# A hybrid decoder layer on one core: eight instead of six row pairs by Strassen's seven products in the first half of each down product

## The chip, the cores and the metric

The kernel runs on one core of a Trainium2 chip. The metric is the device time of one execution in microseconds, from the first to the last instruction with what lies around them; the median of several runs is compared. TensorE does the matrix products, VectorE and ScalarE the elementwise work, GpSimd (POOL in the profile) and SyncE (SP) issue transfers. Each engine takes its own instructions in the order in which they are written.

## The reference

One layer of a decoder for 256 tokens of width 2048, in fp32. What matters here are its two feed-forward blocks:

```
h = h + 0.5 * rmsnorm(swiglu(rmsnorm(h, n_pre), w_gu, w_down), n_post)

def swiglu(x, w_gu, w_down):
    g, u = split(x @ w_gu, 2)
    return (silu(g) * u) @ w_down
```

w_gu is 2048 x 11264 and w_down 5632 x 2048. Between the two blocks stands a mixer (gated linear attention, gated delta rule and cross-attention to 256 memory tokens), which the change does not touch.

## The kernel before, in words

**Units.** A weight matrix is read in units: 256 rows by 512 columns, 512 KB, which land in one of eight places of `raw`. ScalarE rounds a unit into `whi` (L1289, four places), VectorE subtracts that from `raw` and leaves the rest in `wlo` (L1823 for one unit, L1971 for two at once; `wlo` lies over `raw`). Activations are held in the same two parts. An fp32 product is then three matmuls: high by high, high by low, low by high (L858).

**Pairs.** The down product makes 256 tokens x 2048 columns from 5632 = 44 x 128 rows. Its first half makes columns 0 to 1023, the second half the rest. In the first half the rows are taken as 22 pairs (pair q: row blocks 2q and 2q+1), and a pair has two units, one for each 512 columns. In a plain pair, `eight` in the code, the 2 x 2 blocks of activations and the 2 x 2 blocks of weights give eight block products of 128 x 128 x 512, 24 matmuls. In a pair named in `DOWN_AT`, `seven` in the code, they are combined after Strassen: seven block products, 21 matmuls. For that VectorE must form three sums of weight blocks (`weight_sums`, L1959 to L1964, into `wsum`; the third changes a block of `raw` in place), which are rounded and split like a unit (`wsum_hi` L1419, `wsum_lo` L1986), and four sums of activation blocks (`down_sides`, L2110 to L2117, by way of `down_a` into `down_side`), which ScalarE rounds (`down_hi`, L1497) and VectorE splits (`down_sides_lower`, L2122). `down_hi` and `down_lo` keep a place for every seven of the product.

The gate-up products are built alike, with sevens at pairs 2, 4 and 6 of eight (`SEVEN_AT`); their activation sums are made once for all, and not in every step.

**Order.** The order is written out by hand. While TensorE works on unit j (slot j; slots 2q and 2q+1 belong to pair q), the other engines prepare unit j+4, that is pair q+2. ScalarE in slot j waits until unit j is used, rounds unit j+4, and after the rounding of an even slot may do `down_hi`. VectorE splits both units of a plain pair together in the odd slot. The sums for a seven at pair q fall as follows:

```
down_sides(q)         VectorE, slot 2(q-3), ahead of the split of pair q-1
down_hi               ScalarE, slot 2(q-3), behind the first rounding of pair q-1
down_sides_lower      VectorE, slot 2(q-3)+1, behind the split of pair q-1
weight_sums(q)        VectorE, slot 2(q-2), once the preceding seven has used wsum
splits, wsum_lo(q)    VectorE, slots 2(q-2) and 2(q-2)+1
```

In slot 9 VectorE also makes the low part of the last activations (L2066). After the last seven, ScalarE copies the first product out of its bank (`copy_first`, L1426) into the token buffer `nat`, and VectorE combines the banks there.

**The last half.** The second half of the first down product uses plain units only. The second half of the second one takes its pairs in `LAST_ORDER`, the first 14 as pairs, with sevens at places 2, 4, ... 12 of that order (`LAST_AT`), and uses the `down_hi` and `down_lo` that the first half left.

Of the kernel before, what the change touches and what calls it, by code (L numbers as in the profile page):

```python
# [8 lines left out]
SEQ = 256  # L9
P = 128  # L10
NT = SEQ // P
D_FF = ((8 * D // 3 + 255) // 256) * 256
CW = 512
UK = 2
# [33 lines left out]
N_GU = D_FF // CW  # L48
# [39 lines left out]
TURN_AT, UPPER_AT, LOWER_AT = 4, 11, 12  # L88
SEVEN_AT = (2, 4, 6)
N7 = len(SEVEN_AT)  # L90
DOWN_AT = (4, 7, 10, 13, 16, 19)
D7 = len(DOWN_AT)
SIDES_AHEAD = 3
LAST_ORDER = (0, 1, 4, 2, 7, 3, 10, 5, 13, 6, 16, 8, 19, 9, 11, 12, 14, 15, 17, 18, 20, 21)
LAST_PAIRS = 14
LAST_AT = tuple(LAST_ORDER.index(k) for k in DOWN_AT)
LAST_REST = U_F - LAST_PAIRS
LAST_GATE = 2 * LAST_PAIRS + LAST_REST
SPLIT_SMALL = 20
# [9 lines left out]
def hybrid_layer(nc, a, out, h_dram, mk_dram, mv_dram):  # L109
    fp32 = mybir.dt.float32  # L110
    f32r = mybir.dt.float32r
# [6 lines left out]
    with ExitStack() as ctx:  # L118
# [22 lines left out]
        def sem(name):  # L141
            if name not in sems:
                sems[name] = ctx.enter_context(nc.semaphore(name))
            return sems[name]
# [7 lines left out]
        def in_group(name, g=0):  # L152

            if name in ACT_GROUP:
# [4 lines left out]
        ov = overlay([("raw", [P, RAW, UK, CW], fp32)], [("wlo", [P, RAW, UK, CW], f32r)])  # L159
        raw, wlo = ov["raw"], ov["wlo"]  # L160
        ov = overlay(
            [("act_hi", [P, KT_F, SEQ], f32r), ("act_lo", [P, KT_F, SEQ], f32r)],
            [("u_hi", [P, KT_D, SEQ], f32r), ("u_lo", [P, KT_D, SEQ], f32r),
             ("o_hi", [P, 3, KT_O, SEQ], f32r), ("o_lo", [P, 3, KT_O, SEQ], f32r),
             ("msum", [P, NT, CW], fp32), ("mtmp", [P, NT, CW], fp32)],
            [("below", [P, 2 * KT_D, SEQ], fp32), ("mkn", [P, NT, CW], fp32), ("mvn", [P, NT, CW], fp32),
             ("mkT", [P, 4, SEQ], fp32), ("wsm", [P, KT_D, 32], fp32), ("wsm2", [P, KT_D, 64], f32r),
             ("small_T", [64, SEQ], fp32)],
            [("below_post", [P, 80, SEQ], fp32), ("post_a", [P, 2, CW], fp32)],
# [21 lines left out]
             ("mkh", [P, 2, SEQ], fp32), ("mvh", [P, 2, 256], fp32)],  # L191
            [("zbh", U4, f32r), ("zbl", U4, f32r), ("gap", [P, 8, P], fp32), ("sqh", [P, 8, P], f32r)],
            [("sql", [P, 8, P], f32r)],
            [("down_hi", [P, D7, 4, P], f32r), ("down_lo", [P, D7, 4, P], f32r), ("down_a", [P, 2, UK, SEQ], fp32),
             ("down_side", [P, 2, 4, P], fp32)],
            [("res_ffn2", [P, NT, D], fp32), ("post_ffn2", [P, D], fp32)])
        zbh, zbl, sqh, sql = (ov[k] for k in ("zbh", "zbl", "sqh", "sql"))
        x_hi, x_lo = ov["x_hi"], ov["x_lo"]
        down_hi, down_lo, down_a, down_side = (ov[k] for k in ("down_hi", "down_lo", "down_a", "down_side"))
        m_turned, m_swapped = ov["m_turned"][:, :], ov["m_swapped"][:, :]  # L200

        block_res, block_post = (None, res_mix, ov["res_ffn2"]), (None, post_mix, ov["post_ffn2"])
# [6 lines left out]
        ov = overlay(  # L209
            [("nat", [P, NT, D], fp32), ("res", [P, 2, NT, CW], fp32)],  # L210
            [("pr", [P, 4, NT, CW], fp32), ("yr", [P, 10, SEQ], fp32)],
            [("gates", [P, 6, NT, CW], fp32)],
            [("below_wsum", [P, NT, D], fp32), ("wsum", [P, 3, CW], fp32), ("wsum_hi", [P, 3, CW], f32r)],
            [("below_norms", [P, 26, SEQ], fp32), ("gnorm", [P, GLA_DV], fp32), ("dnorm", [P, GDN_D], fp32)],
            [("below_side", [P, NT, D], fp32), ("below_side2", [P, 3, CW], fp32), ("side", [P, N7, 4, P], fp32)],
            [("below_wsl", [P, NT, D], fp32), ("wsum_lo", [P, 3, CW], f32r)])
        nat, res, pr, yr, gates = (ov[k] for k in ("nat", "res", "pr", "yr", "gates"))
        wsum, wsum_hi, wsum_lo = ov["wsum"], ov["wsum_hi"], ov["wsum_lo"]
        gnorm, dnorm, side = ov["gnorm"], ov["dnorm"], ov["side"]

        turned, swapped = nat[:, 0, D // 2:D], nat[:, 1, D // 2:D]

# [8 lines left out]
        def gate_t(t, h=0):  # L231
            return nat[:, t, 2 * h * CW:(2 * h + 1) * CW]
# [4 lines left out]
        def last_unit(j):  # L237

            if j < 2 * LAST_PAIRS:
                return LAST_ORDER[j // 2], j % 2  # L240
            c, r = divmod(j - 2 * LAST_PAIRS, LAST_REST)
            return LAST_ORDER[LAST_PAIRS + r], c

# [21 lines left out]
        def halves(v, l, h):  # L265
# [42 lines left out]
        ov = overlay([("junk", [P, CW], mybir.dt.bfloat16)], [("lrT", [RANK, SEQ], fp32)],  # L308
                     [("last_side_hi", [P, P], f32r), ("last_side_lo", [P, P], f32r)])
# [47 lines left out]
        def at(base, i, per, j):  # L357

            return base + i * per + j
# [9 lines left out]
        def sevens(f, i, s, per, j):  # L369

            if isinstance(i, int) and i > N_GU:
                return (f * ((N_GU - 1) * N7 + D7) + (N_GU - 1) * N7 + D7 * (i - N_GU) + s) * per + j
            return at((f * ((N_GU - 1) * N7 + D7) - N7) * per, i, N7 * per, s * per + j)
# [171 lines left out]
        def _(pl):  # L545
# [31 lines left out]
            for l in range(7):  # L577
                m = 1 << l
# [9 lines left out]
            for l in range(1, 7):  # L588
                m = 1 << l
# [157 lines left out]

            for n in range(N_GU, 2 * N_GU):
                swap_act(n)
            pl.wait_ge(sem("sum_used"), sevens(1, N_GU + 1, D7 - 1, 1, 1))  # L750
            fetch_block(2, a["n_ffn2_post"])
            rsqrt(R_D2, True, 0)
            rsqrt(R_D2, True, 1)
# [3 lines left out]
        def _(pe):  # L757
# [166 lines left out]
            def down_pairs(f, second=False):  # L924
# [21 lines left out]
                if f and second:  # L946
                    pair_stage(f, N_GU + 1, LAST_PAIRS, lambda j: base + 2 * U_F + j, act_hi, act_lo, LAST_AT, side_of,
                               LAST_ORDER, 2 * U_F, False)
                    for j in range(2 * LAST_PAIRS, 2 * U_F - SKEW):
# [7 lines left out]
                pe.wait_ge(sem("act_lo"), (f + 1) * N_GU)  # L957
                pair_stage(f, N_GU, U_F, lambda j: base + j, act_hi, act_lo, DOWN_AT, side_of)

# [317 lines left out]
        def _(ac):  # L1277
# [143 lines left out]
            def copy_first(f, i, n, h=0):  # L1421

                ac.wait_ge(unit_used, n + 1)
                if h == 0:
                    ac.wait_ge(sem("product"), at(f * N_GU, i, 1, 0))
                act(gate_t(0, h), mix[:, 0, :], ACT.Copy).then_inc(sem("first_copied"), 1)  # L1426

            def quads(f, i):
# [21 lines left out]
            def down(f):  # L1450
                n0, q = UB[f"down{f + 1}"], QB[f"down{f + 1}"] // 2

                def tasks(j):
# [15 lines left out]
                    if f == 1 and i == 1 and j in (5, 8):  # L1469

                        ac.wait_ge(acc_out[j // 8], q + 1)
                        squares(R_D2, j // 8, nat[:, :, j // 8 * CW:(j // 8 + 1) * CW])
                    if f == 1 and i == 1 and j == 2 * LAST_AT[-1]:
                        copy_first(f, N_GU + 1, n0 + 2 * U_F + j, 1)
# [16 lines left out]
                for j in range(2 * U_F):  # L1491
                    split_pairs(f, N_GU, DOWN_AT, n0 + j, (0, n0, 2 * U_F), j)
                    tasks(j)
                    if j % 2 == 0 and j // 2 + SIDES_AHEAD in DOWN_AT:
                        e = DOWN_AT.index(j // 2 + SIDES_AHEAD)
                        ac.wait_ge(sem("side"), 5 * (D7 + 1) * f + 5 * (e + 2))
# [7 lines left out]
                for j in range(2 * U_F):  # L1504
                    if j + LOOK < 2 * U_F:
                        split_pairs(f, N_GU + 1, LAST_AT, n0 + 2 * U_F + j, (0, n0, 2 * U_F), j)
                    tasks(j)
# [308 lines left out]
        def _(ve):  # L1816
# [171 lines left out]
            def first_sums(f, i, s, h):  # L1988

                ve.wait_ge(sem("sum_used"), sevens(f, i, s, 1, 1))  # L1990
                ve.wait_ge(sem("first_copied"), per_chunk(f, i, 1, 1))
                tt(up_t(0, h), mix[:, 2, :], gate_t(0, h), ALU.subtract).then_inc(sem("combined"), 1)
                ve.wait_ge(sem("combined"), per_chunk(f, i, 4, 1))
                tt(gate_t(1, h), mix[:, 3, :], up_t(0, h), ALU.add).then_inc(sem("combined"), 1)
# [138 lines left out]
            def last_tasks(j):  # L2133

                n0, q, i = UB["down2"] + 2 * U_F, QB["down2"] // 2, N_GU + 1
                if j == 2 * LAST_AT[-1] + 2:
                    first_sums(1, i, D7 - 1, 1)
                if j == 2 * LAST_AT[-1] + 3:
                    ve.wait_ge(sem("combined"), per_chunk(1, i, 4, 2))
                    tt(up_t(1, 1), mix[:, 1, :], gate_t(1, 1), ALU.add).then_inc(sem("combined"), 1)  # L2140
                    tt(up_t(0, 1), mix[:, 1, :], up_t(0, 1), ALU.add).then_inc(sem("combined"), 1)
                if j in (LAST_GATE - 4, LAST_GATE - 2):
                    scale_product((j - LAST_GATE + 4) // 2)
                if j == LAST_GATE - 1:
                    ve.wait_ge(unit_used, n0 + j + 1)
                    ve.wait_ge(sem("combined"), per_chunk(1, i, 4, 4))
                    tt(gate_t(0, 1), acc[:, 0, 0, :], gate_t(0, 1), ALU.add)
                    tt(gate_t(1, 1), acc[:, 0, 1, :], gate_t(1, 1), ALU.subtract).then_inc(acc_out[0], 1)
                if j == LAST_GATE + 1:
                    ve.wait_ge(acc_out[0], q + 2)  # L2150
                    scale_product(2)
# [10 lines left out]
            def down(f):  # L2162
# [41 lines left out]
                for j in range(2 * U_F):  # L2204
                    tasks(j)
                    if j + LOOK < 2 * U_F:
                        split_pairs(f, N_GU + 1, LAST_AT, n0 + 2 * U_F + j, 2 * U_F + j, (n0 + 2 * U_F + j + LOOK) // RAW + 1, j)

# [428 lines left out]
```

## Time and profile before

| | |
|---|---|
| median of 3 runs | 2433.98 us (2432.99 to 2436.94) |
| the profiled execution's own time | 2433.06 us |
| its span, first to last instruction | 2431.3 us |
| TensorE busy | 2410.6 us, 10933 matmuls |
| VectorE busy | 1840.5 us |
| ScalarE busy | 1336.8 us |
| mean granted clock | 0.999 |

The profile gives times in microseconds from the start of the span. L858 is line 858 of the kernel. Where a row ends in square brackets, the engine stood idle that long ahead of the instruction, until the one named released it. Matmuls overlap: a row shows the latency of one, and the distance between starts is what it takes of TensorE's time.

### The profile page before, as it was taken

What the parts mean: (1) busy time and instruction counts of PE and PEld (TensorE: products, weight loads), DVE (VectorE), ACT (ScalarE), POOL (GpSimd) and SP (SyncE); (2) the same over time, 40 slices, a digit from 0 to 9 for tenths busy, and PEclk for the clock granted to TensorE, in tenths of its full rate; (3) what the DMA queues carried; (4) which work ended last, traced back from release to release, by engine and by line L of the source; (5) the groups of instructions that cost most, each with busy time, mean ns of one, the idle gap of its engine ahead of it and who ended that gap; (6) DMA issues with size and microseconds to landing.
All of it is one profiled execution on the core that took longest, in us unless ns stands there. A gap on an engine that the chain in (4) does not pass through costs nothing.

```text
span 2431.3 us, 32326 instructions
## 1 busy us (share of the span) xinstructions
PE 2410.6 (99%) x10933; PEld 1998.5 (82%) x10933; DVE 1840.5 (76%) x2219; ACT 1336.8 (55%) x1613; POOL 440.0 (18%) x867
## 2 busy tenths in 40 slices
PE   8999999999999999999999999999999999999998
PEld 7888888888888888888888888888888888888886
DVE  6999999987566456677676464465689999998885
ACT  6555555554555556657575444444655555555553
POOL 5211212201222003223242020010112121121000
PEclk9999999999999999999999999999999999999999
DMA  7777767767778765555665677676667777676665
GB/s 243 213 215 214 221 207 218 213 208 223 226 240 257 199 188 157 170 160 159 170 183 159 200 208 195 211 238 191 209 207 220 211 215 217 208 223 211 197 204 193
DMA packets 306063, 498.53 MB, mean 205 GB/s; under 512 B 28460, under 2 KB 102320, under 8 KB 305200
## 3 DMA queue, kind: packets, MB, share of 16 engines
q1 hardware_dynamic: 282336, 457.85, 62.7%
q0 software_dynamic: 23344, 38.95, 5.0%
q8 instruction: 52, 0.85, 0.1%
q10 hardware_dynamic: 288, 0.52, 0.1%
q14 instruction: 43, 0.35, 0.0%
HBM read 471.39 MB, written 8.52 MB: 197 GB/s over the span
## 4 chain that ended last, share of the span: by engine, by line
PE 92%; POOL 2%; DMA 2%; DVE 2%; SPq 1%; issue 1%; ACT 0%; DVEq 0%; POOLq 0%; ACTq 0%
PE acc L770 40%; PE acc L858 39%; PE mix L858 9%; POOL mkh L733 1%; DMA sq<-mk_scratch 1%; POOL mkh L730 1%; PE acc L795 1%; DMA post_a<-n_ffn_post 1%; SPq L438 0%; SPq L472 0%; PE mix L1082 0%; DVE wlo L1971 0%; PE acc L813 0%; PE mix L831 0%; PE mix L1128 0%
## 5 line engine op out<-in xcount | busy, mean ns | idle before, releaser
L1289 ACT ACTIVATE whi<-raw 128x1024 fp32r<-128x1024 f32 x860 | 902.3, 1056 | 972.4 <-PE acc L770 480.0
L1823 DVE TENSOR_TENSOR wlo<-raw,whi 128x1024 fp32r<-128x1024 f32 x568 | 687.3, 1228 | 322.8 <-ACT whi L1289 312.2
L1971 DVE TENSOR_TENSOR wlo<-raw,whi 128x2048 fp32r<-128x2048 f32 x146 | 333.6, 2285 | 54.1 <-ACT whi L1289 54.1
L770 PE MATMUL acc<-whi,u_hi 128*128 128x512 f32 x896 | 356.9, 398 | 0.0
L770 PE MATMUL acc<-whi,u_lo 128*128 128x512 f32 x896 | 349.4, 390 | 0.0
L770 PE MATMUL acc<-wlo,u_hi 128*128 128x512 f32 x896 | 349.1, 390 | 0.0
L387 POOL DMA_DIRECT2D nat<-nat x416 | 203.5, 498 | 791.9 <-DVE nat L2058 649.0
L858 PE MATMUL acc<-whi,x_hi 128*128 128x512 f32 x860 | 334.7, 389 | 0.3 <-DVE nat L1926 0.3
L858 PE MATMUL acc<-wlo,x_hi 128*128 128x512 f32 x860 | 334.6, 389 | 0.0
L858 PE MATMUL acc<-whi,x_lo 128*128 128x512 f32 x860 | 334.6, 389 | 0.0
L770 PEld LDWEIGHTS acc<-whi,u_lo 128*128 128x128 f32 x896 | 168.2, 188 | 35.8
L770 PEld LDWEIGHTS acc<-whi,u_hi 128*128 128x128 f32 x896 | 168.4, 188 | 33.8 <-issue 1.3
L770 PEld LDWEIGHTS acc<-wlo,u_hi 128*128 128x128 f32 x896 | 168.5, 188 | 32.8
L858 PEld LDWEIGHTS acc<-whi,x_hi 128*128 128x128 f32 x860 | 161.4, 188 | 34.4 <-issue 1.1
L858 PEld LDWEIGHTS acc<-wlo,x_hi 128*128 128x128 f32 x860 | 161.4, 188 | 33.7
L858 PEld LDWEIGHTS acc<-whi,x_lo 128*128 128x128 f32 x860 | 161.4, 188 | 33.4
L858 PE MATMUL acc<-whi,act_hi 128*128 128x512 f32 x402 | 156.6, 390 | 1.0 <-DVE wlo L1971 0.9
L858 PE MATMUL acc<-whi,act_lo 128*128 128x512 f32 x402 | 156.4, 389 | 0.0
L858 PE MATMUL acc<-wlo,act_hi 128*128 128x512 f32 x402 | 156.4, 389 | 0.0
L1986 DVE TENSOR_TENSOR wsum_lo<-wsum,wsum_hi 128x1536 fp32r<-128x1536 f32 x78 | 136.6, 1751 | 0.0
L770 PE MATMUL acc<-whi,x_hi 128*128 128x512 f32 x336 | 131.5, 391 | 0.0
L770 PE MATMUL acc<-whi,x_lo 128*128 128x512 f32 x336 | 130.8, 389 | 0.0
(476 smaller groups left out, 3848.7 us busy)
## 6 DMA issues: line engine op xcount, KB each, us to landing
raw<-w_ffn_gu SPq DMA_DIRECT2D x352, 512.0 KB
raw<-w_ffn_down SPq DMA_DIRECT2D x176, 512.0 KB
raw<-w_in SPq DMA_DIRECT2D x224, 256.0 KB
raw<-w_in SPq DMA_DIRECT2D x96, 512.0 KB
raw<-w_mem_kv SPq DMA_DIRECT2D x32, 512.0 KB
raw<-w_out SPq DMA_DIRECT2D x32, 512.0 KB
nat<-nat POOLq DMA_DIRECT2D x416, 32.0 KB, 3.5
raw<-w_in SPq DMA_DIRECT2D x64, 128.0 KB
```

The costliest lines, as they stand in the source:

```text
L387: nc.gpsimd.dma_start(dst[32 * j:32 * j + 32, q * 256:(q + 1) * 256], src[32 * q:32 * q + 32, j * 256:(j + 1) * 256]).then_inc(done, 16)
L730: pl.tensor_tensor(term[:, :, i + 1:], lrow[:, i + 1:, :, i].rearrange("p r u -> p u r"), xcol[:, :, i:i + 1].broadcast_to([P, 4, BLOCK - ...
L733: pl.tensor_tensor(xcol[:, :, i + 1:], xcol[:, :, i + 1:], term[:, :, i + 1:], ALU.subtract).then_inc(sem("substituted"), 1)
L770: ins = nc.tensor.matmul(acc[:, par, t, :], x[:, k0 + k, cols], w[:, k, :], start=first and k == 0 and m == 0, stop=last and k == UK - 1 a ...
L795: ins = nc.tensor.matmul(acc[:, 0, t, :], x[:, UK * j + k, t * P:(t + 1) * P], w[:, j, k, :], start=j == 0 and k == 0 and m == 0, stop=False)
L858: ins = nc.tensor.matmul(bank, sides[a], weights[b], start=start and m == 0, stop=stop and m == 2)
L1289: act(whi[:, l % RING], raw[:, l], ACT.Copy).then_inc(hi_ready, 1)
L1823: tt(wlo[:, l], raw[:, l], whi[:, l % RING].bitcast(fp32), ALU.subtract).then_inc(lo_ready, 1)
L1971: tt(wlo[:, g:g + 2], raw[:, g:g + 2], whi[:, g % RING:g % RING + 2].bitcast(fp32), ALU.subtract).then_inc(lo_ready, 2)
L1986: tt(wsum_lo[:, :, :], wsum[:, :, :], wsum_hi[:, :, :].bitcast(fp32), ALU.subtract).then_inc(sem("sum_lo"), 1)
```

## The change

The first half of each down product has eight sevens instead of six: pairs 4, 6, 8, 10, 13, 15, 17 and 19 instead of 4, 7, 10, 13, 16 and 19. The number of kept activation sums, `D7`, follows. The last half of the second product keeps six sevens, the first six of the new list, at the same places of its order (`L7` = 6); its order names other rows. The temporary `down_a` and `down_side` leave the buffer that they shared with `down_hi` and `down_lo` and lie in the token buffer `nat`, in the columns of which gate and up products are kept between the steps. Since `copy_first` writes there, it waits first until all low activation sums have been made.

```
--- before.py
+++ after.py
@@ -88,12 +88,13 @@
 TURN_AT, UPPER_AT, LOWER_AT = 4, 11, 12
 SEVEN_AT = (2, 4, 6)
 N7 = len(SEVEN_AT)
-DOWN_AT = (4, 7, 10, 13, 16, 19)
+DOWN_AT = (4, 6, 8, 10, 13, 15, 17, 19)
 D7 = len(DOWN_AT)
 SIDES_AHEAD = 3
-LAST_ORDER = (0, 1, 4, 2, 7, 3, 10, 5, 13, 6, 16, 8, 19, 9, 11, 12, 14, 15, 17, 18, 20, 21)
+LAST_ORDER = (0, 1, 4, 2, 6, 3, 8, 5, 10, 7, 13, 9, 15, 11, 12, 14, 16, 17, 18, 19, 20, 21)
 LAST_PAIRS = 14
-LAST_AT = tuple(LAST_ORDER.index(k) for k in DOWN_AT)
+LAST_AT = tuple(LAST_ORDER.index(k) for k in DOWN_AT[:6])
+L7 = len(LAST_AT)
 LAST_REST = U_F - LAST_PAIRS
 LAST_GATE = 2 * LAST_PAIRS + LAST_REST
 SPLIT_SMALL = 20
@@ -191,12 +192,11 @@
              ("mkh", [P, 2, SEQ], fp32), ("mvh", [P, 2, 256], fp32)],
             [("zbh", U4, f32r), ("zbl", U4, f32r), ("gap", [P, 8, P], fp32), ("sqh", [P, 8, P], f32r)],
             [("sql", [P, 8, P], f32r)],
-            [("down_hi", [P, D7, 4, P], f32r), ("down_lo", [P, D7, 4, P], f32r), ("down_a", [P, 2, UK, SEQ], fp32),
-             ("down_side", [P, 2, 4, P], fp32)],
+            [("down_hi", [P, D7, 4, P], f32r), ("down_lo", [P, D7, 4, P], f32r)],
             [("res_ffn2", [P, NT, D], fp32), ("post_ffn2", [P, D], fp32)])
         zbh, zbl, sqh, sql = (ov[k] for k in ("zbh", "zbl", "sqh", "sql"))
         x_hi, x_lo = ov["x_hi"], ov["x_lo"]
-        down_hi, down_lo, down_a, down_side = (ov[k] for k in ("down_hi", "down_lo", "down_a", "down_side"))
+        down_hi, down_lo = ov["down_hi"], ov["down_lo"]
         m_turned, m_swapped = ov["m_turned"][:, :], ov["m_swapped"][:, :]
 
         block_res, block_post = (None, res_mix, ov["res_ffn2"]), (None, post_mix, ov["post_ffn2"])
@@ -217,6 +217,9 @@
         nat, res, pr, yr, gates = (ov[k] for k in ("nat", "res", "pr", "yr", "gates"))
         wsum, wsum_hi, wsum_lo = ov["wsum"], ov["wsum_hi"], ov["wsum_lo"]
         gnorm, dnorm, side = ov["gnorm"], ov["dnorm"], ov["side"]
+
+        down_a = nat[:, 0, 0:2 * CW].rearrange("p (e k n) -> p e k n", e=2, k=UK)
+        down_side = nat[:, 1, 0:2 * CW].rearrange("p (e m n) -> p e m n", e=2, m=4)
 
         turned, swapped = nat[:, 0, D // 2:D], nat[:, 1, D // 2:D]
 
@@ -747,7 +750,7 @@
 
             for n in range(N_GU, 2 * N_GU):
                 swap_act(n)
-            pl.wait_ge(sem("sum_used"), sevens(1, N_GU + 1, D7 - 1, 1, 1))
+            pl.wait_ge(sem("sum_used"), sevens(1, N_GU + 1, L7 - 1, 1, 1))
             fetch_block(2, a["n_ffn2_post"])
             rsqrt(R_D2, True, 0)
             rsqrt(R_D2, True, 1)
@@ -1423,6 +1426,8 @@
                 ac.wait_ge(unit_used, n + 1)
                 if h == 0:
                     ac.wait_ge(sem("product"), at(f * N_GU, i, 1, 0))
+                    if i is N_GU:
+                        ac.wait_ge(sem("down_lo"), (f + 1) * D7)
                 act(gate_t(0, h), mix[:, 0, :], ACT.Copy).then_inc(sem("first_copied"), 1)
 
             def quads(f, i):
@@ -2134,7 +2139,7 @@
 
                 n0, q, i = UB["down2"] + 2 * U_F, QB["down2"] // 2, N_GU + 1
                 if j == 2 * LAST_AT[-1] + 2:
-                    first_sums(1, i, D7 - 1, 1)
+                    first_sums(1, i, L7 - 1, 1)
                 if j == 2 * LAST_AT[-1] + 3:
                     ve.wait_ge(sem("combined"), per_chunk(1, i, 4, 2))
                     tt(up_t(1, 1), mix[:, 1, :], gate_t(1, 1), ALU.add).then_inc(sem("combined"), 1)
```

## Rows read from the trace of the kernel before

**Rows 1.** The page: busy time, share and instructions; granted TensorE clock in 40 slices.
```profile
PE 2410.6 (99%) x10933; PEld 1998.5 (82%) x10933; DVE 1840.5 (76%) x2219; ACT 1336.8 (55%) x1613; POOL 440.0 (18%) x867
...
PEclk9999999999999999999999999999999999999999
```

**Rows 2.** The waits of TensorE: total us, times, longest us.
```profile
PE mix L1128 <- DVE sq L2358: 3.5, 4, 1.9
...
PE acc L858 <- DVE wlo L1971: 0.9, 1, 0.9
```

**Rows 3.** The chain that ended last, first down product: start us, us, what, count.
```profile
498.72 11.56 PE acc L858 x51
```

**Rows 4.** Timeline of TensorE there: start us, us, instruction. First of pairs 4, 5, 7.
```profile
494.48 0.39 PE L858 MATMUL mix<-whi,act_hi 128*128 128x512 f32 x1
...
499.24 0.39 PE L858 MATMUL acc<-whi,act_hi 128*128 128x512 f32 x1
...
510.12 0.39 PE L858 MATMUL mix<-whi,act_hi 128*128 128x512 f32 x1
```

**Rows 5.** Timeline of VectorE: end of a gate-up step, then the first down product.
```profile
441.91 1.75 DVE L1986 TENSOR_TENSOR wsum_lo<-wsum,wsum_hi 128x1536 fp32r<-128x1536 f32 x1
443.58 2.28 DVE L1971 TENSOR_TENSOR wlo<-raw,whi 128x2048 fp32r<-128x2048 f32 x1
...
493.10 1.75 DVE L1986 TENSOR_TENSOR wsum_lo<-wsum,wsum_hi 128x1536 fp32r<-128x1536 f32 x1
...
499.76 1.22 DVE L2066 TENSOR_TENSOR act_lo<-nat,act_hi 128x1024 fp32r<-128x1024 f32 x1
...
513.75 0.68 DVE L2110 TENSOR_TENSOR down_a<-act_hi,act_lo 128x512 f32<-128x512 f32 x1
...
517.21 2.29 DVE L1971 TENSOR_TENSOR wlo<-raw,whi 128x2048 fp32r<-128x2048 f32 x1 [1.72 <-ACT whi L1289]
519.41 0.69 DVE L2122 TENSOR_TENSOR down_lo<-down_side,down_hi 128x512 fp32r<-128x512 f32 x1
520.02 0.68 DVE L1959 TENSOR_TENSOR wsum<-raw 128x512 f32<-128x512 f32 x1
...
522.66 2.36 DVE L1823 TENSOR_TENSOR wlo<-raw,whi 128x1024 fp32r<-128x1024 f32 x2
524.94 1.75 DVE L1986 TENSOR_TENSOR wsum_lo<-wsum,wsum_hi 128x1536 fp32r<-128x1536 f32 x1
```

**Rows 6.** Timeline of ScalarE in the same slot.
```profile
515.52 0.63 ACT L1497 ACTIVATE down_hi<-down_side 128x512 fp32r<-128x512 f32 x1 [2.73 <-DVE down_side L2117]
516.06 1.04 ACT L1289 ACTIVATE whi<-raw 128x1024 fp32r<-128x1024 f32 x1
```

**Rows 7.** The chain in the second down product, a split and the matmuls that waited for it.
```profile
2329.28 2.31 DVE wlo L1971
2331.63 5.75 PE acc L858 x24
```

**Rows 8.** Timeline, second down product: last preparation for its first seven, and that seven.
```profile
2210.17 1.75 DVE L1986 TENSOR_TENSOR wsum_lo<-wsum,wsum_hi 128x1536 fp32r<-128x1536 f32 x1
...
2211.64 0.39 PE L858 MATMUL mix<-whi,act_hi 128*128 128x512 f32 x1
```

**Rows 9.** Timeline of VectorE: an instruction that writes the token buffer.
```profile
586.51 0.68 DVE L2004 TENSOR_TENSOR nat<-acc,nat 128x512 f32<-128x512 f32 x1
```

**Rows 10.** Timeline of VectorE, last half of the second down product.
```profile
2321.42 0.69 DVE L1959 TENSOR_TENSOR wsum<-raw 128x512 f32<-128x512 f32 x1 [1.34 <-PE acc L858]
```

**Rows 11.** Busy time in the first half of the first down product; DMA share last but one.
```profile
core 0: us, PE busy (x) PEld busy (x) DVE busy (x) ACT busy (x) POOL busy (x), PEclk, DMA share, GB/s
472.70:588.40 115.70, 115.70 (x511) 95.56 (x509) 97.63 (x108) 59.35 (x59) 9.29 (x18) 1.00 0.70 214
```

**Rows 12.** Timeline of TensorE at the start of the kernel.
```profile
10.26 0.63 PE L795 MATMUL acc<-wlo,x_hi 128*128 128x512 f32 x1
...
11.96 0.41 PE L795 MATMUL acc<-whi,x_lo 128*128 128x512 f32 x1
```

More of the change, by code:

```diff
@@ L90 @@
 N7 = len(SEVEN_AT)
-DOWN_AT = (4, 7, 10, 13, 16, 19)
+DOWN_AT = (4, 6, 8, 10, 13, 15, 17, 19)
 D7 = len(DOWN_AT)
 SIDES_AHEAD = 3
-LAST_ORDER = (0, 1, 4, 2, 7, 3, 10, 5, 13, 6, 16, 8, 19, 9, 11, 12, 14, 15, 17, 18, 20, 21)
+LAST_ORDER = (0, 1, 4, 2, 6, 3, 8, 5, 10, 7, 13, 9, 15, 11, 12, 14, 16, 17, 18, 19, 20, 21)
 LAST_PAIRS = 14
-LAST_AT = tuple(LAST_ORDER.index(k) for k in DOWN_AT)
+LAST_AT = tuple(LAST_ORDER.index(k) for k in DOWN_AT[:6])
+L7 = len(LAST_AT)
 LAST_REST = U_F - LAST_PAIRS
@@ L193, in hybrid_layer @@
             [("sql", [P, 8, P], f32r)],
-            [("down_hi", [P, D7, 4, P], f32r), ("down_lo", [P, D7, 4, P], f32r), ("down_a", [P, 2, UK, SEQ], fp32),
-             ("down_side", [P, 2, 4, P], fp32)],
+            [("down_hi", [P, D7, 4, P], f32r), ("down_lo", [P, D7, 4, P], f32r)],
             [("res_ffn2", [P, NT, D], fp32), ("post_ffn2", [P, D], fp32)])
@@ L198, in hybrid_layer @@
         x_hi, x_lo = ov["x_hi"], ov["x_lo"]
-        down_hi, down_lo, down_a, down_side = (ov[k] for k in ("down_hi", "down_lo", "down_a", "down_side"))
+        down_hi, down_lo = ov["down_hi"], ov["down_lo"]
         m_turned, m_swapped = ov["m_turned"][:, :], ov["m_swapped"][:, :]
@@ L219, in hybrid_layer @@
         gnorm, dnorm, side = ov["gnorm"], ov["dnorm"], ov["side"]
+        down_a = nat[:, 0, 0:2 * CW].rearrange("p (e k n) -> p e k n", e=2, k=UK)
+        down_side = nat[:, 1, 0:2 * CW].rearrange("p (e m n) -> p e m n", e=2, m=4)
         turned, swapped = nat[:, 0, D // 2:D], nat[:, 1, D // 2:D]
@@ L749, in _ @@
                 swap_act(n)
-            pl.wait_ge(sem("sum_used"), sevens(1, N_GU + 1, D7 - 1, 1, 1))
+            pl.wait_ge(sem("sum_used"), sevens(1, N_GU + 1, L7 - 1, 1, 1))
             fetch_block(2, a["n_ffn2_post"])
@@ L1425, in copy_first @@
                     ac.wait_ge(sem("product"), at(f * N_GU, i, 1, 0))
+                    if i is N_GU:
+                        ac.wait_ge(sem("down_lo"), (f + 1) * D7)
                 act(gate_t(0, h), mix[:, 0, :], ACT.Copy).then_inc(sem("first_copied"), 1)
@@ L2136, in last_tasks @@
                 if j == 2 * LAST_AT[-1] + 2:
-                    first_sums(1, i, D7 - 1, 1)
+                    first_sums(1, i, L7 - 1, 1)
                 if j == 2 * LAST_AT[-1] + 3:
```

## The prediction, made before the changed kernel had run

> **What bounds the kernel now.** I read the page first [rows 1]. TensorE is busy 99% of the span and its granted clock is at full speed in all forty slices; VectorE is at 76%. So time is removed only by giving TensorE fewer matmuls, and time is added wherever TensorE stands still. The list of what TensorE waited for comes next [rows 2]: its first line is 3.5 us, in the mixer, where the longest single wait is 1.9, and one wait of 0.9 us in the last down product, the largest in which weights came late to the pair stages. So every microsecond of idle that the change brings will be new.
>
> Then the first half of the first down product. The chain of waits [rows 3] is TensorE alone: the row shown is 51 matmuls in 11.56 us, three of a seven and the 48 of two eights. From the timeline [rows 4] the pattern repeats every 510.12 - 494.48 = 15.64 us; 48 matmuls take 510.12 - 499.24 = 10.88 us, so one is 0.2267 us; an eight is 5.44 us and a seven 499.24 - 494.48 = 4.76 us. (The 0.39 us of a row is its latency, not its share.) The reader is to see there that consecutive matmuls start without a gap.
>
> Last, VectorE and ScalarE in the same stretch [rows 5, 6]. They are what the change loads.
>
> **Part 1, what is removed.** Pairs 6, 8, 15 and 17 become sevens and 7 and 16 become eights: two sevens more per first half, three matmuls less for each. 2 x 3 x 0.2267 = 1.36 us per down product, 2.72 us in both. That is the whole gain that is possible.
>
> **Part 2, what is added on VectorE and ScalarE, and in which order.** The queues are strictly in order. A seven at pair q makes VectorE form the activation sums (L2110 to L2117) in slot pair q-3 and, after ScalarE's rounding (L1497), their low part (L2122); in slot pair q-2 it forms the weight sums. With sevens three pairs apart those two jobs fall in different slot pairs with a pair of slack. With sevens two pairs apart, VectorE alternates: weight sums for q, then activation sums for q+2 and the plain split of pair q+1. One lap is, from starts of rows [rows 5]:
> - weight sums, 520.02 to 522.66: 2.64 us;
> - two single splits, to 524.94: 2.28 us;
> - low part of the weight sums until the next instruction can start: 443.58 - 441.91 = 1.67 us;
> - activation sums to the start of the plain pair split, 513.75 to 517.21: 3.46 us. Only 1.74 of it is VectorE's work: the row at 517.21 shows 1.72 of idle, for ScalarE. The reason: ScalarE's down_hi stands in its queue ahead of the second weight rounding of that pair and cannot start before the sums are there (515.52), the rounding follows at 516.06, and the pair split needs it [rows 6];
> - pair split 2.20 (517.21 to 519.41), low activation part 0.61 (to 520.02).
>
> Together 12.86 us. In that time TensorE has one seven and one eight, 10.20 us. So TensorE must wait 2.66 us per lap, and always at the same place: before the eight that follows a seven, for wlo of L1971.
>
> **Part 3, the stalls one by one** (DOWN_AT is 4, 6, 8, 10, then 13, 15, 17, 19, two runs). The pair split is ready 1.67 + 3.46 + 2.29 = 7.42 us after the start of the preceding wsum_lo. The one such wait of the trace shows the rest [rows 7]: the split ends at 2331.59, TensorE starts 0.04 us later, and its next 24 matmuls take 5.75 us where 5.44 is the rule, so a restart costs 0.31 us beside the idle.
> - Pair 5: wsum_lo starts at 493.10 [rows 5], ready 500.52; TensorE gets there at 499.24 [rows 4]. Idle 1.32, cost 1.63.
> - Pair 7: one lap later plus the low part of the last activations (L2066), which falls into this lap at slot 9: 1.22 us [rows 5], 1.14 with the same 0.08 overlap as the other instructions. Ready 514.52. TensorE is through seven 6 at 499.24 + 1.63 + 10.20 = 511.07. Idle 3.49, cost 3.80.
> - Pair 9: ready 527.38, TensorE at 525.07. Idle 2.35, cost 2.66.
> - Pair 14: between 10 and 13 the old spacing gives the slack back. Weight sums start 9.90 us after the preceding seven's start (510.12 to 520.02), so pair 14 is ready 9.90 + 4.92 (sums and two splits) + 7.42 = 22.24 after seven 10's start, TensorE is there after 15.64 + 4.76 = 20.40. Idle 1.88, cost 2.19.
> - Pairs 16 and 18: 2.66 each.
>
> Sum 15.60, less 1.36: +14.24 us per down product. The second product stands the same way: wsum_lo of its first seven at 2210.17, the seven at 2211.64 [rows 8], a lead of 1.47 us against 1.38 in the first, so I take the same. Both: +28.5 us.
>
> **Part 4, edits costed at nothing.** down_a and down_side move into the token buffer. VectorE instructions of 128x512 that write it (L2004 and its like) take 0.68 us, as does L2110 in the old place [rows 5, 9]; I take 0, and 0.1 us in each of some 12 laps, 1.2 in all, as the upper end. ScalarE's new wait for down_lo before copying the first product stands at slot 38; the last down_lo is issued in slot 33, five slots (over 12 us) earlier; behind it stand only weight roundings, so without that cover each 0.1 us would be one of a later split. The last half of the second product keeps six sevens at places 2, 4, ... 12 of its order. There sevens already stand two pairs apart, without activation sums, and TensorE stood still for weights once before the last loads [rows 2, 7]: VectorE even waits 1.34 us for TensorE there before its weight sums [rows 10]. That is the best evidence that two-pair spacing alone is cheap, and that the activation sums in between are what costs. The weight loads stay 8 units ahead, with the DMA at 0.70 of its engines in this stage [rows 11], and are asked for more slowly than now.
>
> **Bounds.** The restart: none (the loop of Part 2 is VectorE's, so only the first stall of each run and the long one would shrink, about 0.4 us per product) up to the slow start of the kernel, where matmuls from 10.26 to 11.96 start 0.42 us apart [rows 12]; six like that are 1.2 us instead of 0.31, and again this counts at pairs 5 and 14 only: +1.8 per product. With the 1.2 us of Part 4, +27.5 to +33.5.
>
> **The sum.** Span 2431.3 + 28.5 = 2459.8; the profiled execution's own time 2433.06 becomes 2461.5. The median shown, 2433.98, lies 0.9 above it: 2462.
>
> **Rivals.**
> - *No stall: two engines have slack enough.* 76% of VectorE speaks for it, and the last half with two-pair spacing. It decides if a lap is at most 10.20 us; the rows say 12.86, and VectorE's work alone 11.14. Time 2434.0 - 2.7 = 2431 (0.1% less, within what counts as no change). Chance 0.04.
> - *VectorE's work alone bounds.* If ScalarE's rounding were not held behind down_hi, a lap would be 12.86 - 1.72 = 11.14. Stalls then: none at 5, 1.97 at 7, 0.93 at 9, 0.46 at 14, 0.93 twice, 5.2 less 1.36 = 3.9 per product: 2442. Against it: the 1.72 us of that wait is there already before each plain split that follows activation sums [rows 5]. Chance 0.05.
> - *The clock falls in the gaps.* No stretch of this trace is below full speed, and its idle times of TensorE reach 1.9 us inside the kernel [rows 2]; the new ones are 2.35 and, once per product, 3.49. If the engine went to its lower level (1.2 instead of 2.4 GHz) after the 3.49 alone, for the 45 matmuls up to the next stall, they would take 20.4 us where the lap allows 12.86: +7.5 per product, 2477. Chance 0.05.
>
> The Trainium skill speaks for that last rival: its page "TensorE: Matmul & The Clock Gate", section "HAM oscillation — how this bites in real kernels", says that waits between bursts of matmuls can bring the engine back to its lower clock, each time anew. No run shown here has such a wait, so the trace neither agrees nor disagrees.
>
> **How the numbers follow.** My forecast, the laps of Part 2, has 0.84; 0.02 is left for what I have not seen. Forecast: 2462, its own range 2461 to 2468 by the bounds. The range for 8 in 10 is 2455 to 2469: the forecast's bounds, and 6 us below for one stall per product being smaller than worked out. A measurement of this kernel tells about 0.2% (4.9 us) from no change. Slower 0.95 (forecast, VectorE alone, clock, most of the rest), the same 0.04 (no stall), faster 0.01: the gain possible is 2.7 us.
>
> **What would show it.** In the profile after: TensorE waits on VectorE's wlo of L1971 (its new line) some 12 times, 28 us with the restarts, the longest 3.5 us, twice; in the chain VectorE and ScalarE appear between TensorE's pieces in both first halves; start to start of the weight sums in a run 12.9 us; weight roundings behind down_hi. TensorE has 12 matmuls fewer. The prediction is wrong if TensorE's waits there stay under 10 us, if they are for down_lo or sum_lo rather than wlo, or if the granted clock drops.

## The result, and the profile after

| | before | changed |
|---|---|---|
| median | 2433.51 us | 2462.12 us (2460.22 to 2462.96, 4 runs) |
| span of the profiled execution | 2431.3 us | 2459.8 us |
| first seven to the second half's first matmul, first product | 94.25 us | 108.25 us |
| first seven to the last half's first seven, second product | 104.72 us | 120.15 us |

The changed kernel takes 1.0115 times the time of before, 95% interval 1.0101 to 1.0129. Lines are moved: L861 is L858 of before, L1976 is L1971, L1964 to L1969 are L1959 to L1964, L1991 is L1986, L2115 to L2122 are L2110 to L2117, L2127 is L2122, L1292 is L1289, L1502 is L1497, L1828 is L1823, L1131 is L1128 and L1251 is L1248.

The page of the changed kernel: busy time, the granted clock, and the shares of the chain that ended last.

```profile
PE 2416.2 (98%) x10921; PEld 1997.9 (81%) x10921; DVE 1866.0 (76%) x2267; ACT 1342.3 (55%) x1621; POOL 439.5 (18%) x867
...
PEclk9999999999999999999999999999999999999999
...
PE 85%; DVE 7%; issue 3%; POOL 2%; DMA 1%; ACT 1%; SPq 1%; DVEq 0%; ACTq 0%; POOLq 0%
```

TensorE makes 12 matmuls fewer and is busy a little longer [rows 1]. The page of before has the chain as TensorE for 92% and VectorE for 2%; now they are 85% and 7%. The waits of TensorE (total us, times, longest us):

```profile
PE acc L861 <- DVE wlo L1976: 24.4, 13, 3.3
PE mix L1251 <- DMA vec<-n_ffn_pre: 3.1, 1, 3.1
PE mix L1131 <- DVE sq L2363: 2.9, 3, 1.6
```

One of the thirteen in the first line was there before [rows 2]. The other twelve are new, six in either product, 23.5 us of idle. These are the six of the first product, in the timeline of TensorE; the number in brackets is the idle time ahead of the matmul:

```profile
500.45 0.50 PE L861 MATMUL acc<-whi,act_hi 128*128 128x512 f32 x1 [1.17 <-DVE wlo L1976]
...
514.44 0.50 PE L861 MATMUL acc<-whi,act_hi 128*128 128x512 f32 x1 [3.34 <-DVE wlo L1976]
...
527.31 0.50 PE L861 MATMUL acc<-whi,act_hi 128*128 128x512 f32 x1 [0.76 <-DVE wlo L1976]
...
555.24 0.50 PE L861 MATMUL acc<-whi,act_hi 128*128 128x512 f32 x1 [1.78 <-DVE wlo L1976]
...
568.11 0.50 PE L861 MATMUL acc<-whi,act_hi 128*128 128x512 f32 x1 [0.75 <-DVE wlo L1976]
...
580.98 0.50 PE L861 MATMUL acc<-whi,act_hi 128*128 128x512 f32 x1 [2.37 <-DVE wlo L1976]
```

The reader is to see the distances: 12.87 us from the second to the third, and again from the fourth to the fifth to the sixth. TensorE is paced by something that takes 12.87 us. The timeline of VectorE shows what:

```profile
506.98 1.75 DVE L1991 TENSOR_TENSOR wsum_lo<-wsum,wsum_hi 128x1536 fp32r<-128x1536 f32 x1
508.65 0.68 DVE L2115 TENSOR_TENSOR nat<-act_hi,act_lo 128x512 f32<-128x512 f32 x1
...
512.10 2.29 DVE L1976 TENSOR_TENSOR wlo<-raw,whi 128x2048 fp32r<-128x2048 f32 x1 [1.71 <-ACT whi L1292]
514.31 0.69 DVE L2127 TENSOR_TENSOR down_lo<-nat,down_hi 128x512 fp32r<-128x512 f32 x1
514.91 0.69 DVE L1964 TENSOR_TENSOR wsum<-raw 128x512 f32<-128x512 f32 x1
...
517.56 2.36 DVE L1828 TENSOR_TENSOR wlo<-raw,whi 128x1024 fp32r<-128x1024 f32 x2
519.84 1.75 DVE L1991 TENSOR_TENSOR wsum_lo<-wsum,wsum_hi 128x1536 fp32r<-128x1536 f32 x1
521.51 0.69 DVE L2115 TENSOR_TENSOR nat<-act_hi,act_lo 128x512 f32<-128x512 f32 x1
...
524.96 2.29 DVE L1976 TENSOR_TENSOR wlo<-raw,whi 128x2048 fp32r<-128x2048 f32 x1 [1.72 <-ACT whi L1292]
527.17 0.69 DVE L2127 TENSOR_TENSOR down_lo<-nat,down_hi 128x512 fp32r<-128x512 f32 x1
527.78 0.69 DVE L1964 TENSOR_TENSOR wsum<-raw 128x512 f32<-128x512 f32 x1
```

From the weight sums at 514.91 to the next at 527.78 are 12.87 us, and VectorE has no idle time but one: 1.72 us ahead of the paired split at 524.96, for ScalarE. ScalarE meanwhile:

```profile
523.28 0.63 ACT L1502 ACTIVATE down_hi<-nat 128x512 fp32r<-128x512 f32 x1 [2.94 <-DVE nat L2122]
523.82 1.99 ACT L1292 ACTIVATE whi<-raw 128x1024 fp32r<-128x1024 f32 x2
```

It rounds the activation sums first, waits 2.94 us to do so, and only then rounds the two units of weights that VectorE's split needs.

### The profile page after: what moved, and what is told of

Read it like the earlier page. It is cut to its first block, busy times and chain, and to the rows that moved or that the text cites. A ratio compares the mean times of both kernels' runs of the same rounds, so it can differ in the third digit from the quotient of the medians.

```text
span 2459.8 us, 32366 instructions
## 1 busy us (share of the span) xinstructions
PE 2416.2 (98%) x10921; PEld 1997.9 (81%) x10921; DVE 1866.0 (76%) x2267; ACT 1342.3 (55%) x1621; POOL 439.5 (18%) x867
## 4 chain that ended last, share of the span: by engine, by line
PE 85%; DVE 7%; issue 3%; POOL 2%; DMA 1%; ACT 1%; SPq 1%; DVEq 0%; ACTq 0%; POOLq 0%
PE acc L773 41%; PE acc L861 33%; PE mix L861 8%; DVE wlo L1976 1%; DVE wlo L1828 1%; ACT whi L1292 1%; POOL mkh L736 1%; DVE wsum_lo L1991 1%; POOL mkh L733 1%; PE acc L798 1%; DMA sq<-mk_scratch 1%; SPq L441 0%; DVE wsum L1969 0%; PE mix L834 0%; DVE wsum L1964 0%
## 5 line engine op out<-in xcount | busy, mean ns | idle before, releaser
L1292 ACT ACTIVATE whi<-raw 128x1024 fp32r<-128x1024 f32 x860 | 900.6, 1056 | 978.3 <-PE acc L773 479.7
L1828 DVE TENSOR_TENSOR wlo<-raw,whi 128x1024 fp32r<-128x1024 f32 x576 | 696.9, 1228 | 323.2 <-ACT whi L1292 312.6
L1976 DVE TENSOR_TENSOR wlo<-raw,whi 128x2048 fp32r<-128x2048 f32 x142 | 324.4, 2285 | 57.6 <-ACT whi L1292 57.6
L861 PE MATMUL acc<-whi,x_hi 128*128 128x512 f32 x860 | 334.7, 389 | 0.3 <-DVE nat L1931 0.3
L861 PE MATMUL acc<-whi,x_lo 128*128 128x512 f32 x860 | 334.6, 389 | 0.0
L861 PE MATMUL acc<-wlo,x_hi 128*128 128x512 f32 x860 | 334.6, 389 | 0.0
L861 PEld LDWEIGHTS acc<-whi,x_hi 128*128 128x128 f32 x860 | 161.4, 188 | 34.5 <-issue 1.1
L861 PEld LDWEIGHTS acc<-whi,x_lo 128*128 128x128 f32 x860 | 161.4, 188 | 33.6
L861 PEld LDWEIGHTS acc<-wlo,x_hi 128*128 128x128 f32 x860 | 161.4, 188 | 33.5
L861 PE MATMUL acc<-whi,act_hi 128*128 128x512 f32 x374 | 149.3, 399 | 24.5 <-DVE wlo L1976 24.4
L861 PE MATMUL acc<-whi,act_lo 128*128 128x512 f32 x374 | 147.4, 394 | 0.0
L861 PE MATMUL acc<-wlo,act_hi 128*128 128x512 f32 x374 | 147.4, 394 | 0.0
L1991 DVE TENSOR_TENSOR wsum_lo<-wsum,wsum_hi 128x1536 fp32r<-128x1536 f32 x82 | 143.6, 1751 | 0.0
```

Of the source, the lines that this page charges most:

```text
L861: ins = nc.tensor.matmul(bank, sides[a], weights[b], start=start and m == 0, stop=stop and m == 2)
L1292: act(whi[:, l % RING], raw[:, l], ACT.Copy).then_inc(hi_ready, 1)
L1828: tt(wlo[:, l], raw[:, l], whi[:, l % RING].bitcast(fp32), ALU.subtract).then_inc(lo_ready, 1)
L1976: tt(wlo[:, g:g + 2], raw[:, g:g + 2], whi[:, g % RING:g % RING + 2].bitcast(fp32), ALU.subtract).then_inc(lo_ready, 2)
L1991: tt(wsum_lo[:, :, :], wsum[:, :, :], wsum_hi[:, :, :].bitcast(fp32), ALU.subtract).then_inc(sem("sum_lo"), 1)
```

## The experiments

Times are compared by the distances of the table above, taken in each run's trace from the same two matmuls; they leave out what lies between the two products, with the mixer in it. That stretch took from 1.0 us less to 1.8 us more than in the trace of before; in e1, e3, e4 and e7 TensorE's granted clock fell once in it, behind a wait of 1.9 to 2.3 us in the mixer. Each experiment starts from the changed kernel.

**ScalarE's rounding one slot later** (e1_round_later).

```
-                    if j % 2 == 0 and j // 2 + SIDES_AHEAD in DOWN_AT:
+                    if j % 2 == 1 and j // 2 + SIDES_AHEAD in DOWN_AT:
                         e = DOWN_AT.index(j // 2 + SIDES_AHEAD)
                         ac.wait_ge(sem("side"), ...)
                         act(down_hi[:, e], ...)
```

> ScalarE rounds the activation sums (down_hi) one slot later, behind the second weight rounding of that pair and no longer ahead of it; nothing else differs from the changed kernel. My theory (the lap is VectorE and ScalarE handing over to each other, 12.86 us): the 1.72 us of VectorE's wait goes out of each lap, which becomes 11.14 us, VectorE's own work. TensorE then stands still 0.62 us and restarts for 0.31 before pairs 9, 16 and 18, 1.8 to 2.1 before pair 7, not at all before 5 and 14: +3.5 us per product against the kernel before, about 2440.5 us, span 2438.3. Rival, the weights' transfers or the place of the temporary sums make the stalls: 2462 as now. Rival, the two-pair spacing alone makes them: 2462 as now.

Median 2439.66 us, ratio 1.0027 (1.0018 to 1.0037); +3.23 us in the first product and +3.23 in the second. VectorE:

```profile
511.96 0.69 DVE L1964 TENSOR_TENSOR wsum<-raw 128x512 f32<-128x512 f32 x1
...
518.55 0.69 DVE L2115 TENSOR_TENSOR nat<-act_hi,act_lo 128x512 f32<-128x512 f32 x1
...
520.22 2.29 DVE L1976 TENSOR_TENSOR wlo<-raw,whi 128x2048 fp32r<-128x2048 f32 x1
...
523.02 0.69 DVE L1964 TENSOR_TENSOR wsum<-raw 128x512 f32<-128x512 f32 x1
```

The lap is 523.02 - 511.96 = 11.06 us and the split at 520.22 stands right behind the sums, with no idle. Moving one instruction of 0.63 us gave back 22.5 of 28.6 us. What stays is VectorE's own work against TensorE's 10.20 us. TensorE's waits for the split, eight new ones and the one of before:

```profile
PE acc L861 <- DVE wlo L1976: 7.3, 9, 1.5
```

In either product they are 0.57, 0.54 and 0.57 us before pairs 9, 16 and 18, where I had 0.62, and 1.51 before pair 7, where I had 1.8 to 2.1.

**The buffer move alone** (e2_move_alone): `DOWN_AT` and `LAST_ORDER` as before, the rest as changed.

> The changed kernel with the six sevens of before (4, 7, 10, 13, 16, 19) and their old order in the last half: what is left of the change is the temporary sums in the token buffer and ScalarE's added wait. My theory: both cost nothing, 2433.5 within 0.5 us of span (2431.3). Rival, the move or the wait costs something: more by at least 1.2 us of span (0.1 us in each of 12 places), up to 28 if it is the whole cause.

2432.76 us against 2432.27 in the same runs, ratio 1.0001 (0.9992 to 1.0011), span 2430.8, 94.25 us in the first product and 104.72 in the second, to the hundredth what they were. With six sevens, place and wait cost nothing. This alone doesn't clear the place in the denser order, since here a small cost would vanish in the slack (e8, below). There the rows do: the first activation sum takes 0.68 us in the changed kernel as before, and the lap worked out from rows of the old place, 12.86 us, is the one measured, 12.87. The wait is clear there too: ScalarE's copy of the first product starts at 589.15, and the last low activation sum ended at 581.52.

**Activation sums once per product** (e3_sums_once). This kernel leaves out seven of the eight sets of activation sums of each product, so its output is not the layer's; only its time is of use. ScalarE's rounding and `down_sides_lower` are cut down in the same way as `down_sides`.

```
-                    if j % 2 == 0 and j // 2 + SIDES_AHEAD in DOWN_AT:
+                    if j == 2 * (DOWN_AT[0] - SIDES_AHEAD):
                         down_sides(f, ...)
...
-                    return down_hi[:, s, m, :], down_lo[:, s, m, :]
+                    return down_hi[:, 0, m, :], down_lo[:, 0, m, :]
```

> The eight sevens, but the activation sums are made, rounded and split once per product, for its first seven, and every other seven of the product uses these: seven eighths of that work left out, matmuls and weight sums as in the changed kernel. My theory: a VectorE lap of 8.79 us is under the 10.20 of TensorE, so only the lap that also holds L2071 comes near (0.3 us), and the gain of 1.36 per product is paid out: about -1.0 us per product, 2431.4 us, span 2429.2. Rival, two-pair spacing with its weight sums is itself too dense: still above 2450.

2432.05 us against 2432.27, ratio 0.9996 (0.9986 to 1.0005): by the measured time it is not to be told from the kernel before. By the trace it is -1.03 us in either product, and the stretch between them 1.6 us longer. The line of the waits is what it was before the change:

```profile
PE acc L861 <- DVE wlo L1976: 0.9, 1, 0.9
```

So eight sevens two pairs apart, with all their weight sums, don't make TensorE wait for the split, and within the products the gain is paid out nearly whole (1.03 of 1.36 us). The stalls come with the activation sums between them.

**The activation sums on GpSimd** (e4_pool_sums): `pool_sides` has the five instructions of `down_sides` for e = 1 to 7, each set waiting for `down_lo` of the set two before; VectorE makes only the first.

```
+                for e in range(1, D7):
+                    ...
+                    if e > 1:
+                        pl.wait_ge(sem("down_lo"), f * D7 + e - 1)
+                    pl.tensor_tensor(a, act_hi[...], act_lo[...], ALU.add).then_inc(sem("side"), 1)
```

> The eight sevens with all their work, but GpSimd, idle in this stage, forms the activation sums of all sevens but the first of each product; ScalarE and VectorE round and split them as before. My theory: the lap of VectorE is 2.64 + 2.28 + 1.67 + 2.20 + 0.61 = 9.40 us, below 10.20; with 1.14 us of L2071 in one lap about 1 us is lost once per product: 2431.5 to 2433 us, if GpSimd makes a set within 10.2 us (its 128x512 instructions took 1.0 to 2.3 us before, small ones 0.6 to 0.8, so about 5 us). Rival, GpSimd's instructions slow VectorE's with two inputs down, or come late: a VectorE lap above 10.2 us, 2435 to 2450 us.

2445.84 us, ratio 1.005 (1.0033 to 1.0066): the rival. Both engines' rows, in order of time:

```profile
515.10 0.68 DVE L1984 TENSOR_TENSOR wsum<-raw 128x512 f32<-128x512 f32 x1
...
515.32 1.60 POOL L650 TENSOR_TENSOR nat<-act_hi,act_lo 128x512 f32<-128x512 f32 x1 [6.83 <-DVE down_lo L2147]
...
515.81 1.66 DVE L1986 TENSOR_TENSOR wsum<-wsum,raw 128x512 f32<-128x512 f32 x1
...
517.39 0.94 DVE L1987 TENSOR_TENSOR raw<-raw 128x512 f32<-128x512 f32 x1
...
517.75 0.91 POOL L653 TENSOR_TENSOR nat<-nat 128x128 f32<-128x128 f32 x1
...
526.49 0.69 DVE L1984 TENSOR_TENSOR wsum<-raw 128x512 f32<-128x512 f32 x1
```

VectorE's L1984 here is the first instruction of the weight sums and L1986 the second, 0.69 us in the kernel before; L650 to L657 are GpSimd's five. Beside GpSimd's first instruction L1986 takes 1.66, the next one (L1987) 0.94 instead of 0.68, and the two splits behind the sums 2.77 instead of 2.36. The lap, 526.49 - 515.10, is 11.39 us and not 9.40: what was taken off VectorE came back as slower instructions of its own.

**Short distances one at a time** (e5_single_gaps): `DOWN_AT = (4, 7, 9, 12, 14, 17, 19)`, and `LAST_ORDER` to match.

> Seven sevens at 4, 7, 9, 12, 14, 17, 19: the distance of two pairs comes three times per product, never twice in a row, and the temporary sums and all else are as in the changed kernel. My theory: a distance of two costs what pair 14 cost in my working, 1.88 us of idle and 0.31 of restart, even alone: three times 2.19 less 0.68 for one more seven is +5.9 us per product, +11.8 in all, ratio 1.005, with TensorE's waits for the paired split six times at about 1.9 us. Rival, VectorE's work alone (11.14 us a lap): an isolated short distance costs 0.46 at most, +0.7 per product, ratio 1.001.

2448.8 us, ratio 1.0064 (1.0049 to 1.0079); +9.12 us in the first product and +7.11 in the second. The waits are where and as long as expected, 1.7 to 2.1 us each. But look at the 24 matmuls behind each, in the chain of the first product:

```profile
517.44 7.35 PE acc L861 x24
...
546.92 5.73 PE acc L861 x24
...
574.86 7.39 PE acc L861 x24
```

The second takes 5.73 us, much as in [rows 7] (5.75); the first and the third take 7.35 and 7.39. Two slow restarts of 1.6 us more are the 3.2 us between 5.9 and 9.1; in the second product it was one of three, behind the wait of 1.80 us at 2271.09, and not behind the two of 1.74. A short distance costs a stall even alone, which was the question; its price had a second part that this working had at nothing.

**The same, with the later rounding** (e6_single_gaps_later).

> The same seven sevens, and ScalarE rounds the activation sums behind the second weight rounding of the pair. My theory: the pair split is ready 1.72 us earlier, 20.52 us after the preceding seven's start where TensorE comes at 20.40; the first matmuls of a pair need it no earlier than that, so it stalls by 0.1 us or nothing, and one more seven per product gains 0.68: -0.3 to -0.7 us per product, ratio 0.9995 within the measurement's 0.001, and the first half of either product shorter than before by that in the trace. Rival, any two-pair distance costs a stall: ratio 1.002 or more.

2431.67 us, ratio 0.9995 (0.9986 to 1.0004), -0.68 us in either product: exactly one more seven each, with no wait for the split in either first half. This is the version in which everything that it gains arrives. By the two distances of its trace it is ahead of both kernels; by the measurement of its time it is not to be told from the one before.

**ScalarE's rounding made longer** (e7_round_in_parts, with eight sevens; e8_six_round_in_parts, with the six of before).

```
-                        act(down_hi[:, e], down_side[:, e % 2], ACT.Copy).then_inc(...)
+                        for m in range(4):
+                            ins = act(down_hi[:, e, m, :], down_side[:, e % 2, m, :], ACT.Copy)
+                        ins.then_inc(...)
```

> The changed kernel, but ScalarE rounds each set of activation sums in four instructions of 128x128 instead of one of 128x512: the same result, and by four such in a row at the start of the kernel before (1.12 us) some 0.49 us longer. ScalarE is busy 55% of the span. My theory (ScalarE's rounding is a link of the lap): every lap and every wait for the paired split grows by 0.49, six per product, so +2.9 per product and +5.9 us in all on the changed kernel, 2468, ratio 1.0140 to 1.0145. Rival (ScalarE has slack, VectorE's work alone makes the lap): 2462 unchanged.

> The same four instructions in the kernel with six sevens of before (temporary sums in the token buffer). My theory: with three pairs between sevens the paired split is ready 2.6 us or more ahead of TensorE, so 0.49 more costs nothing: ratio 1.000, no wait for weights in either first half. Rival (the added work costs by itself wherever it stands): +2.9 per product, ratio 1.0024.

With eight sevens 2466.67 us, ratio 1.0138 (1.0122 to 1.0155), span 2464.2: 4.4 us above the changed kernel. With six, ratio 0.9996 (0.9986 to 1.0005), and 94.25 and 104.72 us in the two products, as before. Rows of e7, ScalarE's first (L1503 is L1502), then the starts of VectorE's weight sums (L1966 is L1964), then TensorE's first and last wait of the first product (L1978 is L1976):

```profile
524.12 0.91 ACT L1503 ACTIVATE down_hi<-nat 128x128 fp32r<-128x128 f32 x4 [2.25 <-DVE nat L2124]
524.93 1.99 ACT L1292 ACTIVATE whi<-raw 128x1024 fp32r<-128x1024 f32 x2
```

```profile
515.75 0.68 DVE L1966 TENSOR_TENSOR wsum<-raw 128x512 f32<-128x512 f32 x1
...
528.89 0.69 DVE L1966 TENSOR_TENSOR wsum<-raw 128x512 f32<-128x512 f32 x1
```

```profile
501.01 0.50 PE L861 MATMUL acc<-whi,act_hi 128*128 128x512 f32 x1 [1.75 <-DVE wlo L1978]
...
583.21 0.50 PE L861 MATMUL acc<-whi,act_hi 128*128 128x512 f32 x1 [2.65 <-DVE wlo L1978]
```

The next rounding starts 0.81 us after the first part, not 0.54: 0.27 us more, where I had expected 0.49 from four instructions that read another memory. The lap grows by exactly that, 13.14 - 12.87 = 0.27. The expectation counted six waits per product; but all eight roundings of a product count, since ahead of the waits at pairs 5 and 14 two of them stand one behind the other: from the first seven (494.34 here, 494.36 in the changed kernel) to the wait at pair 5 is 0.58 us more, and to the last wait, at pair 18, 2.25 us more (583.21 against 580.98), eight times 0.28. In the second product it is 2.26 us more to the last wait, but only 0.75 over the whole distance, because the changed kernel lost 1.5 us to a slow restart behind that wait and this one did not. The other 1.5 us of the 4.4 lie between the products, where the clock fell in this execution. So an instruction on an engine that is busy 55% of the span is paid in full in every lap, and not at all where sevens stand three pairs apart.

## Why the prediction was right

**The lap of Part 2** is right to a hundredth: 12.86 worked out, 12.87 measured. Its two halves are shown one by one. The 1.72 us of ScalarE's turn are shown by the move of one instruction (e1: 11.06 where 11.14 was worked out) and by lengthening it (e7); VectorE's own share is shown by e1's lap, which has no idle in it, and by e3, where the stalls are gone with the activation sums. That it was the lap, and not the buffer's place, is shown by e2 together with the unchanged lengths of the rows in the changed kernel.

**The stalls of Part 3.** By the steps of Part 3 TensorE starts pairs 5, 7, 9, 14, 16 and 18 at 500.56 (the split's end and 0.04), 514.56, 527.42, 555.45, 568.31 and 581.17; it started at 500.45, 514.44, 527.31, 555.24, 568.11 and 580.98, up to 0.2 us earlier, of which 0.12 is the earlier start of the first seven. The first product lost 14.00 us where I had 14.24. My list of signs has "28 us with the restarts"; by Part 3's own sums it is twice 15.60, 31.2, and 28 is what remains behind the gain. Measured were 23.5 us of idle, 3.7 of restarts and, as follows, 4.7 of slow matmuls.

**The restart.** 0.31 us was right for most, but not for all, and this is the part of a rival that came true. The granted clock, with busy times, in stretches behind some of the waits (the last three columns are clock, DMA share, GB/s):

```profile
core 0: us, PE busy (x) PEld busy (x) DVE busy (x) ACT busy (x) POOL busy (x), PEclk, DMA share, GB/s
...
517.00:520.00 3.00, 3.00 (x10) 2.38 (x9) 2.96 (x4) 3.00 (x3) 0.00 (x0) 0.66 0.00 0
520.00:525.00 5.00, 5.00 (x23) 4.13 (x23) 3.21 (x7) 2.06 (x4) 0.00 (x0) 1.00 0.70 211
556.00:560.00 4.00, 4.00 (x12) 3.09 (x12) 3.93 (x6) 2.24 (x2) 0.00 (x0) 0.57 0.01 5
...
2244.00:2248.00 4.00, 3.40 (x15) 2.81 (x16) 3.93 (x7) 0.89 (x1) 0.00 (x0) 1.00 0.00 0
2310.00:2314.00 4.00, 2.86 (x7) 2.29 (x8) 3.96 (x6) 0.35 (x1) 0.00 (x0) 0.63 0.28 108
```

Behind three of the twelve waits the mean granted clock of the stretch is 0.57 to 0.66 of full speed; the timeline has some eight matmuls there 0.43 us apart instead of 0.23, which is the lower of TensorE's two levels (1.2 against 2.4 GHz), and then 0.23 again. I had put the fall behind the longest wait alone, and for all 45 matmuls up to the next. It came behind the 3.34 us of the first product, not behind the 3.34 of the second (2244 to 2248), and also behind waits of 1.78 and 2.38. The mixer shows the same: TensorE has a wait of 1.91 us there in e3 and in the kernel before, and the clock fell behind it in e3 (first row) and not before (second row):

```profile
956.00:961.00 5.00, 4.64 (x16) 3.91 (x17) 4.07 (x12) 0.38 (x1) 0.00 (x0) 0.66 0.30 100
...
957.00:962.00 5.00, 4.05 (x23) 3.54 (x24) 4.54 (x13) 0.83 (x3) 0.00 (x0) 1.00 0.38 108
```

The prediction calls itself wrong if the granted clock drops. It did drop, in these three stretches; the page's forty slices are too coarse to show it, and as a cause it is 1.5 of 28.6 us. Nor was it so that no stretch of the trace before was below full speed: [rows 12], at the kernel's start, are matmuls 0.42 us apart, the spacing of the lower level.

The falls agree with the page "TensorE: Matmul & The Clock Gate" of the Trainium skill, section "HAM oscillation — how this bites in real kernels", in that waits between bursts bring the clock down, time and again. They don't agree with it in length: the section goes by waits longer than any of the three here. Which of the waits do it, the length did not tell, and I leave that open.

What it cost depends on where it fell, but not as the bounds had it, which counted a slow start at pairs 5 and 14 alone. VectorE's lap doesn't wait for TensorE, so a slow TensorE uses up idle time that was coming: behind 514.44 the next wait was 0.76 us instead of 2.35, and pair 9 still started at 527.31. The fall behind pair 14 (555.24) cost nothing either: pair 16 started one lap later, at 568.11, behind a wait of 0.75 instead of 2.35. Behind the last wait of a run nothing was coming. By the steps of Part 3 those are pairs 9 and 18, two per product as the bounds had, but other ones; a fall behind pair 18 was seen, none behind pair 9. In the chain of the second product:

```profile
2257.47 5.73 PE acc L861 x24
...
2311.14 7.26 PE acc L861 x24
```

7.26 us for 24 matmuls against 5.73, 1.5 us that stayed. So the second product lost 15.43 us and not 14.24. Against it, the stretch between the two products was 0.9 us shorter in this execution, and the sum, 14.00 + 15.43 - 0.93 = 28.5, came out as worked out by some luck in the last microsecond: the clock's 1.5 us and what the rest was short of cancelled.

**What was costed at nothing** (buffer, wait) cost nothing, as said at e2, and from the first seven of the last half to the end it is 115.0 us in both kernels. The statement of Part 4 that two-pair spacing alone is cheap holds: e3.

**The rivals.** No stall: 12 stalls, and e3 shows the condition under which it would have been so. VectorE's work alone: the case that e1 makes, 3.23 us more per product where this rival had 3.9 and e1's own working 3.5; the lap was 0.08 shorter, the wait before pair 7 was 1.51 us and not 1.8 or more, and before pair 14 there was none, where the rival had a cost of 0.46. The clock: real, but 1.5 us and not 15; it was not behind the longest wait alone, and it lasted for some eight matmuls and not 45.

## What to carry to other kernels

Before making a saving denser, lay out one lap of all engines that prepare for it, with the idle times inside it, and not their busy shares: here VectorE stood at 76% and ScalarE at 55%, and together they took 12.87 us where TensorE had 10.20. When two engines hand work back and forth in order, look at what stands ahead of the instruction that the other waits for: an instruction that nobody needs soon, queued first and waiting itself, makes its neighbour late, and moving it behind cost nothing here. And a saving of one unit of TensorE's work (0.68 us a seven) is less than the smallest of these stalls cost: 0.54 us of idle and 0.31 of restart in e1. So it only pays where the slack is shown.

## What the runs showed of the hardware that I had not expected

- TensorE's granted clock fell behind 3 of the 12 new waits of the changed kernel, at waits of 1.8 to 3.3 us, and in the kernel with single short distances (e5) behind 3 of 6; behind one wait of 1.91 us in the mixer it fell in e3 and e7 and not in the kernel before and e5. Where all of the 24 matmuls that followed were in one piece of the chain, they took 1.5 to 1.7 us more, beside the 0.31 of any restart.
- In e4 VectorE and GpSimd slowed each other when both worked on two tiles in on-chip memory: VectorE's 128x512 sum took 1.66 us instead of 0.69 beside GpSimd's, and a GpSimd instruction of 128x128 up to 2.39 us instead of 0.79.
- Four ScalarE instructions of 128x128 delayed the next one by 0.81 us where one of 128x512 delays it by 0.54: the split into small instructions cost 0.27 us, where rows of instructions with another source had led me to expect 0.49.
